# The last transposes, three output products in turns, and the last norm's factor on one engine: one change to a two-block fp32 kernel

## The reference

```python
def second_block(x, ...):                       # x: [1, 256, 1024], 16 heads of 64
    y = rms_norm(h, attn_norm)
    q, k, v = split(y @ w_qkv)
    o = moba_attention(q, k, v, rel_bias)       # 256 tokens: one causal block per head
    h = h + o @ w_o
    y = rms_norm(h, ffn_norm)
    h = h + conv_ffn(y, w_up, conv_w, conv_b, w_down)
    return rms_norm(h, final_norm)              # h * rsqrt(mean(h*h) + 1e-6) * final_norm
```

## Time and profile before

| what | value |
|---|---|
| median of 3 runs | 935.9 us (927.82, 935.9, 936.33) |
| profiled execution | 936.45 us |
| its span in the trace | 934.4 us |
| mean granted clock of TensorE | 0.986 of full |
| attention and output products, with the two norms around them | 620 to 740 us |
| last norm and output | 924 us to the end |

### The profile page before, as it was taken

How to read it: one execution, slowest core, us unless ns; L and a number is a source line. 1 busy time by engine, 2 the same in 40 slices (tenths; PEclk the granted TensorE clock), 3 DMA queues, 4 the chain that set the end, 5 groups by cost and what they waited for, 6 DMA issues and landing times.

```text
span 934.4 us, 18538 instructions
## 1 busy us (share of the span) xinstructions
PE 892.0 (95%) x7968; PEld 845.4 (90%) x7968; DVE 669.9 (72%) x1131; ACT 504.5 (54%) x811; POOL 64.0 (7%) x86
## 2 busy tenths in 40 slices
PE   5698999999999989999999999999999999999997
PEld 2497898999999989999999999999888999999997
DVE  3878666676888777677888775587666688777653
ACT  2487676543444565555354444466555476566442
POOL 0100000111111000020000000120000100000002
PEclk9799899999999999999999999999999999999999
DMA  8744233233567765455998889635432355545631
GB/s 329 255 186 159 71 134 136 92 136 136 176 218 245 264 221 187 180 199 190 279 342 294 280 289 250 215 103 214 135 137 90 136 180 182 183 186 182 228 125 46
DMA packets 27681, 177.31 MB, mean 190 GB/s; under 512 B 2864, under 2 KB 5680, under 8 KB 7504
## 3 DMA queue, kind: packets, MB, share of 16 engines
q1 hardware_dynamic: 27600, 176.13, 54.0%
HBM read 174.29 MB, written 1.84 MB: 188 GB/s over the span
## 4 chain that ended last, share of the span: by engine, by line
PE 82%; DVE 9%; ACT 6%; DMA 1%; issue 1%; SPq 0%; DVEq 0%; ACTq 0%
PE ps L1091 45%; PE ps L1097 22%; DVE wl L1836 2%; PE ps L1089 2%; DVE acc L1735 1%; PE ps L1136 1%; ACT wh L1449 1%; PE ps L1144 1%; PE ps L1230 1%; PE ps L1247 1%; PE ps L1147 1%; PE ps L1095 1%; DMA raw<-in_ada_dram 1%; DVE KT L1718 1%; DVE tmp L1718 1%
## 5 line engine op out<-in xcount | busy, mean ns | idle before, releaser
L1091 PE MATMUL ps<-HH,wh 128*128 128x256 f32 x1480 | 375.7, 289 | 2.6 <-DVE wl L1836 2.1
L1836 DVE TENSOR_TENSOR wl<-raw,wh 128x1024 fp32r<-128x1024 f32 x265 | 321.6, 1235 | 76.0 <-ACT wh L1449 75.3
L1091 PE MATMUL ps<-HH,wl 128*128 128x256 f32 x1480 | 362.0, 280 | 0.0
L1449 ACT ACTIVATE wh<-raw 128x1024 fp32r<-128x1024 f32 x265 | 273.5, 1042 | 143.5 <-PE ps L1097 111.2
L1091 PEld LDWEIGHTS ps<-HH,wh 128*128 128x128 f32 x1480 | 281.6, 190 | 12.0 <-issue 4.1
L1091 PEld LDWEIGHTS ps<-HH,wl 128*128 128x128 f32 x1480 | 280.6, 190 | 2.1 <-issue 2.1
L1097 PE MATMUL ps<-HL,wh 128*128 128x256 f32 x1480 | 229.3, 280 | 0.0
L1097 PEld LDWEIGHTS ps<-HL,wh 128*128 128x128 f32 x1480 | 197.7, 189 | 0.1
L1091 PE MATMUL ps<-FH,wh 128*128 128x256 f32 x352 | 85.9, 278 | 0.0
L1091 PE MATMUL ps<-FH,wl 128*128 128x256 f32 x352 | 85.9, 278 | 0.0
L1735 DVE SCALAR_TENSOR_TENSOR acc<-raw,silc,acc 128x512 f32<-128x512 f32 x101 | 76.6, 758 | 8.1 <-DMA raw<-in_ada_dram 4.9
(11 more groups left out here) (265 smaller groups left out, 1070.5 us busy)
## 6 DMA issues: line engine op xcount, KB each, us to landing
raw<-in_ada_dram SPq DMA_DIRECT2D x32, 1024.0 KB, 5.3
raw<-in_w_fi_dram SPq DMA_DIRECT2D x22, 1024.0 KB, 4.9
raw<-in_w_up_dram SPq DMA_DIRECT2D x22, 1024.0 KB, 4.8
raw<-in_w_rest_dram SPq DMA_DIRECT2D x20, 1024.0 KB, 4.8
raw<-in_w_in_dram SPq DMA_DIRECT2D x16, 1024.0 KB, 4.9
raw<-in_w_qkv_dram SPq DMA_DIRECT2D x12, 1024.0 KB, 4.8
raw<-in_w_o_dram SPq DMA_DIRECT2D x8, 1024.0 KB, 4.8
raw<-in_w_fo_dram SPq DMA_DIRECT2D x8, 1024.0 KB, 4.9
```

The costliest lines, as they stand in the source:

```text
L1091: e.matmul(o, w[:, k, 128 * t:128 * t + 128], x_hi[:, k0 + k, :], start=first and n + k == 0, **MM)
L1449: e.activation(whl[u % HALF][0][:, 0:n], raw[i % RAW][:, c:c + n], ACT.Copy).then_inc(*a_hi.up(u))
L1836: e.tensor_tensor(wl[:, 0:n], raw[i % RAW][:, c:c + n], wh[:, 0:n].bitcast(F32), ALU.subtract).then_inc(*v_lo.up(u))
```

## The change

Three edits. (1) `attend` yields once more after k 3, so that k 4 and all later steps of that head come a tick later, unless they wait for v2 anyway. (2) wo2 0, 1 and 2 run in turns: units 189, 191, 193, 190, 192, 194; then the three are closed, one after another, and wo2 3 follows. (3) For the last norm ScalarE weighs tiles 0 to 5, VectorE weighs 6 and 7 after they are squared and then multiplies by R in four calls of two tiles, GpSimd does nothing, and SP waits for one event of VectorE for each DMA.

```diff
@@ attend(h)
         for k in range(5):
             emit("att", h, k, st)
             yield
+            if k == 3:
+                yield
@@
     together = {("fg", 0): (high_first, ("fu", 0)), ("q2", 0): (high_first, ("k2", 0)),
-                ("ug", 0): (high_first, ("uv", 0))}
+                ("ug", 0): (high_first, ("uv", 0)), ("wo2", 0): (in_turns, ("wo2", 1), ("wo2", 2))}
@@
-            way, second = together[key]
-            way([p, named[second]])
+            way, *others = together[key]
+            way([p] + [named[other] for other in others])
@@
-    weighed = (1, 3, 5)
+
+    weighed = range(6)
@@ sync_engine
         for j in range(4):
-            for kt in (2 * j, 2 * j + 1):
-                if kt in weighed:
-                    g_norm.wait_ge(e, "final", kt)
-                else:
-                    v_norm.wait_ge(e, "final", kt)
+            v_norm.wait_ge(e, "final", j)
             e.dma_start(out[:, 512 * j:512 * j + 512], flat(X, j)).then_inc(*d_out.up("out"))
@@ vector_engine
             elif kind == "finish":
+                for kt in (6, 7):
+                    a_norm.wait_ge(e, "sq", N5, kt)
+                    e.tensor_scalar(X[:, kt, :], X[:, kt, :], v("final", kt), None, ALU.mult).then_inc(
+                        *v_norm.up("weighed", kt))
                 a_norm.wait_ge(e, "r", N5)
-                for kt in range(8):
-                    if kt not in weighed:
-                        x_ready(e, N5, kt)
-                        e.scalar_tensor_tensor(out=X[:, kt, :], in0=X[:, kt, :], scalar=v("final", kt), in1=R[:, :],
-                                               op0=ALU.mult, op1=ALU.mult).then_inc(*v_norm.up("final", kt))
+                for j in range(4):
+                    for kt in (2 * j, 2 * j + 1):
+                        (a_norm if kt in weighed else v_norm).wait_ge(e, "weighed", kt)
+                    e.tensor_tensor(X[:, 2 * j:2 * j + 2, :], X[:, 2 * j:2 * j + 2, :],
+                                    R[:, None, :].broadcast_to([128, 2, T]), ALU.mult).then_inc(*v_norm.up("final", j))
@@ pool_engine
-            elif kind == "finish":
-                a_norm.wait_ge(e, "r", N5)
-                for kt in weighed:
-                    a_norm.wait_ge(e, "weighed", kt)
-                    e.tensor_tensor(X[:, kt, :], X[:, kt, :], R[:, :], ALU.mult).then_inc(*g_norm.up("final", kt))
```

More of the change, by code:

```diff
@@ L952, in _program @@
         if key in together:
-            way, second = together[key]
-            way([p, named[second]])
+            way, *others = together[key]
+            way([p] + [named[other] for other in others])
             if key == ("q2", 0):
                 begin(third_scale())
-        elif key not in [second for _, second in together.values()]:
+        elif key not in [other for _, *others in together.values() for other in others]:
             for n in range(len(p["units"])):
```

## The result

| | before | after |
|---|---|---|
| median of 20 runs each, us | 929.69 (926.79 to 937.44) | 923.63 (922.03 to 929.88) |
| profiled execution, us | 936.45 | 924.06 |
| span, us | 934.4 | 921.9 |
| mean granted clock | 0.986 | 0.987 |

The ratio is 0.9914, 95% interval 0.9891 to 0.9937: 0.9% faster, with 1% inside the interval. The forecast was 928.7 in a range of 922.0 to 932.5. The sizes don't fit as they stand. The two profiled executions lie 12.4 us apart, the sum was 7.2, and the medians of the 20 runs lie 6.1 apart, since the 17 new runs of before moved its median from 935.9 to 929.69.

The account below looks back on a forecast made before the run. TensorE, busy 95% of the span, was taken to bound the kernel; 2.7 + 3.4 + 1.1 = 7.2 us off the profiled 936.45 is 929.2, less 0.55 over the median gives 928.7 us, range 922.0 to 932.5.

Parts of the forecast that it names:

- the sum: Whole kernel: the gains of the three edits, 2.7 + 3.4 + 1.1 = 7.2 us off the profiled 936.45.
- Rival (d): Whole run: waits between heads close too, or the run falls low like one of 927.82; 920 to 926 us, chance 0.2.
- rival (c): Transposes of groups 1 and 2: TensorE's lead is taken back at the next wait; 2.7 us less gain, 931.4, chance 0.07.
- the `lo` of unit 193: Group 3, first tile after the transposes: TensorE waits for VectorE's low part of the weights, a new wait of 0.35 us.
- the bank: Start of wo2 3: it waits for the bank that the first residual frees, a new wait of 0.2 us.
- the heap on GpSimd: Closing of three products: GpSimd's five additions come together, sum ready about when TensorE wants it; cost 0, bounds 0 and 2.3.
- the clock's fall: Group 3 before: 3.5 us at half rate; if it fell all the same, 1.7 us lost, gain only 1.7.
- Rival (a): Norm after wo2 3: slow GpSimd additions make the sum 2.3 us late; gain 4.9, 931.0 us, chance 0.15.
- rival (b): Transposes and norm: TensorE's clock falls at both, 28 us at half rate cost 14 us; 943 us, chance 0.03.
- The 1.6 us taken for the weights by v: Group 3, after the transposes: weights by v at full clock take 1.6 us, between 1.2 and 2.4.
- the floor's reason: Last norm: four transfers of 256 KB issued 0.61 us apart, no longer 0.85, might queue; gain then only 0.3 us.
- output DMAs that land more than 2.6 us after issue: Kernel end: listed as a profile sign that would make the forecast wrong, there for the last norm's output transfers.

Follow-up runs that it names:

- edit 1's low groups: Faster runs of before plus edit 1, alone or with edit 2: medians 924.6 us (10 runs) and 923.9 us (5 runs).
- a_spread: The kernel after, with each output product closed as soon as its second unit is done: 922.31 us, ratio to before 0.9914.
- a_spread_again: The kernel after with each output product closed as soon as it is done, timed once more: 926.41 us, ratio to before 0.9922.
- the runs with the filling: 14 instead of 9 filling matmuls at norm N4: on before 928.31 us; on after with products closed singly 923.60 and, repeated, 924.10 us.
- filling: Before with four extra matmuls on TensorE ahead of the transposes of head 12: 932.09 us, ratio to before 1.0009.

## Why the prediction was right or wrong

**The base, the step that failed.** "That execution lies 0.55 over the median of the runs, so I predict 928.7": the sum was taken off a profiled execution at the 118 pace, and two of the three runs lie in the upper group with it. At the 113 pace before takes 928.8, and 928.8 - 7.2 would have been 921.6. The prediction used the two levels of the granted clock as all that there is to TensorE's speed, and its "5.44 us a product" as valid throughout; that figure is the 113 pace, and the long stretch of the same trace was never compared with it. Rival (d) allowed for a run that "falls low like the 927.82", without a cause. The base was too high by 7 us and the sum too large by 2, so 928.7 is 5.1 over the 923.63, still in the range. The measured time lies in rival (d)'s band, 920 to 926, given 0.2. That the change came out at 0.9% where 0.8% was said is luck, as the sum was too large and the medians moved by more than the edits gave. In the 40 runs of the result the change at equal pace is 4.5 us, 0.5%; the rest is that 9 of the 20 of before lie in the upper group and 1 of the 20 of after. The chances put most on a change within 1%, where the ratio's middle lies, and could not tell it from 1% with such a base.

**Edit 1**, 2.7 said, 2.3 measured (1.15 a group). The mechanism held: VectorE's wait for TensorE stays the same 4.36 us at the next q2, so TensorE led the cycle, and rival (c) is out. The missing 0.2 a group: behind the transposes the tiles of v2 ran at the 118 pace (L1088, starts 0.12 apart) for four tiles, 48 matmuls of 4.5 ns. At equal pace the gain is the 1.4 a group that was said.

**Edit 2 with edit 1 in group 3**, 3.4 said, 1.85 measured (3.0 less group 2's part, taken as group 1's 1.15). The order, the place of each wait and the clock came as written. Mis-sized: the `lo` of unit 193 cost 0.6, not 0.35; the bank 0.5, not 0.2; the heap on GpSimd, put at nothing, 0.6. a_spread shows the last two to be worth 1.4 with what hangs on them. The bounds counted 1.7 for the clock's fall, which cost 1.0. That 1.0 is part of the 1.85, but the clock stays up in some executions without the turns as well: the turns themselves bring 0.7 to 0.9, 1.1 at equal pace. Unit 190 starts 9.3 us after the end of unit 189's tiles (8.8 said, 6.67 before). Rival (a) had the mechanism, at 0.6 instead of 2.3; rival (b), a clock that falls more, is out. The 1.6 us taken for the weights by v at full clock came as 1.5 (711.26 to 712.76).

**Edit 3**, 1.1 said, 0.6 measured. VectorE and the last issue came as said; the floor's reason decided half of it, that transfers issued 0.61 apart land later. So "output DMAs that land more than 2.6 us after issue" was the right sign to look for.

The terms sum to 2.3 + 1.85 + 0.6 = 4.75 by the profile, against 5.2 by the low groups of all comparisons and 4.5 by those of the result.

**What stays open.** What picks the pace at a break. a_spread and a_spread_again are one kernel; TensorE's starts in the 3 us ahead of the long stretch, counted from its begin, agree within some 0.01 us, and it takes 183.96 us in one and 190.96 in the other. So the program alone doesn't decide it. Why after is in the upper group in 3 of 32 and before in 40 of 124 isn't shown; the runs with the filling only suggest that the way into the stretch bears on it. Whether filling, or edit 1, keeps the clock up in group 3. And the 1.0 us that edit 1's low groups gain beyond its profile.

## What to carry to other kernels

Before you price an edit, check that the profiled execution is typical: compare the distance between starts of one form of matmul in stretches that the edit doesn't touch, and look whether the runs fall in two groups. Before you credit an edit with a clock that stays up, look at a second execution of the old order. Compare two kernels by groups of the same pace, and cut the two traces at common rows before crediting an edit. Running products in turns fills a hole, but close each as it ends: follow-up work in a heap delays the bank and the norm.

## What the hardware showed that I had not expected

- At granted clock 1.00, matmuls of 128x256, each with a weight load of its own and one behind another, start 113.3 to 113.5 or 117.8 ns apart: the 15 traces have 104 unbroken streams of over 100 matmuls at the first pace, 42 at the second, none between, and none that changes on its way. One stream holds its pace over 1577 matmuls, and that is worth 7 us of 930 here. The Trainium skill (TensorE: Matmul & The Clock Gate, section "Part 1: The HAM clock gate") adds some 2.5 ns to the columns' time of each matmul at the open clock. By it 256 columns would start an estimated 109.2 ns apart; no stream here shows that figure, and the measurement decides.
- The granted clock fell to 0.50 for 3.4 us in three of four profiled executions with the same order of work there, and stayed at 1.00 in the fourth. The fall cost 1.0 us.
- Four output transfers of 256 KB issued 0.6 us apart land 2.5 to 3.0 us after issue; 0.85 apart, 2.5 to 2.6.
